# State-space part of the third block: step sizes and decays made once beside the projection, distances on ScalarE, state chain first

## The chip, the cores and the metric

The kernel runs on one core of one Trainium2 chip. The metric is the device time of one execution in microseconds (us), the median of several runs. All data are float32. Five engines work side by side, each through its own instruction queue: TensorE (PE, matmuls), VectorE (DVE), ScalarE (ACT), GpSimd (POOL) and SyncE (SP, which here only issues DMAs).

## The reference, cut to what matters

The program is three blocks after one another on 512 tokens of width 1024. The change lies in the third block, in its bidirectional state-space mixer (`ssd_mixer`): 16 heads of 64 channels, a state of 128, two groups of 8 heads that share the matrices B and C.

```python
xbc = silu(depthwise_conv_centred(xbc, conv_w) + conv_b)        # width 5
y = xh * d_skip
for d in range(2):                                              # forward, backward
    dt = softplus(dt_raw + dt_bias[d]);  a_neg = -exp(a_log[d])
    y = y + ssd_direction(...)                                  # d = 1 on flipped tokens

def step(state, inp):                                           # one chunk of tokens
    cum = cumsum(dt * a_neg)
    seg = cum[t] - cum[s];  decay = exp(seg) where s <= t, else 0
    w = scores[t, s] * decay * dt[s]                            # scores = C B^T
    y_intra = w @ x
    y_inter = (C @ state) * exp(cum)
    state = exp(cum[-1]) * state + (exp(cum[-1] - cum) * dt * x)^T @ B
```

## The kernel before, in words

Channels lie on the 128 partitions and the 512 tokens along the free dimension; the kernel's chunks are P = 128 tokens, so TT = 4 chunks; KT = 8 is both 1024/128 and the number of pairs of heads. Every part is a block: each engine has its instruction list, semaphores order them, and all engines meet at the block's end. Within an engine the order is the one in which the code is written; there is no planner.

`ssd_inputs` makes two norms, then the projection: 20 tiles of 8 matmuls (12 tiles for x, B and C, 8 for the gate z) from weight pieces that `Stream` loads, and one narrow product of 16 columns for `dt_raw` behind them (L2114). ScalarE copies each tile out of PSUM (L2125, L2127), VectorE does the convolution of 5 taps (L2147, L2151), and ScalarE the final Silu (L2132). `ssd_prepare` turns x and B to token-major and makes the scores.

`ssd_direction` runs twice, after that. Its work, on heads in 16 rows first and then on tokens in 128 partitions:

- step sizes and decays: bias, softplus, the running sum by chunk (scan), the rows G (log decay), I (for the state's part of the output), V (weight of a token in the state), in 16x512 tiles, on VectorE with two visits to ScalarE (L2258 to L2310);
- G and I are stored to DRAM (L2238, L2239) and read back broadcast over partitions: one row of G per head into `spread` (L2245), one row of I per head into `ep` (L2251);
- TensorE turns dt, G and V to token-major columns and spreads the chunk decays (L2382, L2385), VectorE copies them out (L2318);
- `xdt` = x times dt, four chunks (L2323); then the chain of three state steps: the weighed input `xw` (L2329), the kept state (L2333), a product per group on TensorE (L2391), and its addition (L2339);
- the pairs of heads: VectorE subtracts the column of G from the spread row and clamps, 4 instructions per head (L2350), ScalarE takes Exp (L2271), VectorE multiplies with the masked scores `gm` (L2371), TensorE makes the state's part (L2400) and the part in the chunk (L2407), VectorE adds both up to y (L2358 to L2360).

VectorE's loop does the differences of pair k + 1, the weights of pair k and the addition of pair k - 1. At the other end of the program, `load_x` loads the small vectors by ScalarE's queue, among them `dt_bias` and `a_log` (L367, L368), and waits for them at its end.

## Time and profile before

| | us |
|---|---|
| median of 3 runs (lowest to highest) | 4182.87 (4182.28 to 4185.58) |
| span of the profiled execution | 4179.0 |
| median less that span | 3.9 |
| projection, first TensorE record to the end of the dt product | 2624.7 to 2771.7 |
| prepare, first to last instruction | 2780.0 to 2788.5 |
| first direction, first to last VectorE instruction | 2788.8 to 2873.5 |
| second direction, first to last VectorE instruction | 2874.1 to 2956.6 |

The profiled execution has no time of its own beside its span; the 3.9 us are what the median of the other runs has over it. Over the whole span TensorE is busy 87%, VectorE 34%, ScalarE 16%. The parts of the program follow each other, so what a part costs is its own length, whatever these shares say.

### The profile page before, as it was taken

The numbers are of one execution on the slowest core, as the hardware profiler recorded it, in microseconds if no ns is written. First come the engines' busy times: TensorE is split into PE (matmuls) and PEld (weight loads), VectorE is DVE, ScalarE is ACT, GpSimd is POOL, SyncE is SP. The second block draws the span as 40 slices with busy tenths as digits, with TensorE's granted clock in tenths as the row PEclk, the third lists the DMA queues.
The fourth block names the chain that finished last, engine by engine and source line by source line (L and its number), as shares of the span: only waits on it lengthen the run. The fifth ranks groups of instructions, "written<-read, shape, count | busy, mean of one in ns | idle before, by whom it ended". The sixth has DMA issues, their size and how long they took to land. (4 is left out here: it accounts for less than half of the span.)

```text
span 4179.0 us, 31843 instructions
## 1 busy us (share of the span) xinstructions
PE 3652.1 (87%) x11526; PEld 1766.0 (42%) x11526; DVE 1431.0 (34%) x2486; ACT 686.6 (16%) x1281; POOL 231.4 (6%) x247
## 2 busy tenths in 40 slices
PE   7998888999794999999999995964899776899998
PEld 2535443443442443434343442433444666444443
DVE  1017622591324212121212124428442788510111
ACT  1012202011102101010101012122171333110000
POOL 0000003000001000000000001000000454000000
PEclk9995798999996999999999997987899888999999
DMA  2225729121116999999999985102221000212220
GB/s 74 70 77 174 251 64 342 64 77 60 51 65 264 371 408 399 408 399 408 399 409 399 408 334 179 57 21 75 96 81 61 6 6 1 101 61 81 81 73 28
DMA packets 218800, 729.49 MB, mean 175 GB/s; under 512 B 16208, under 2 KB 26977, under 8 KB 183879
## 3 DMA queue, kind: packets, MB, share of 16 engines
q1 hardware_dynamic: 178124, 628.30, 39.7%
q10 hardware_dynamic: 28394, 55.66, 3.8%
q0 software_dynamic: 12176, 44.11, 3.0%
q8 instruction: 68, 1.11, 0.1%
q14 instruction: 38, 0.30, 0.0%
HBM read 678.33 MB, written 49.69 MB: 174 GB/s over the span
## 5 line engine op out<-in xcount | busy, mean ns | idle before, releaser
L1739 PE MATMUL bank<-moe_gu,all_hT 128*128 128x512 f32 x1088 | 472.2, 595 | 0.0
L1216 PE MATMUL bank<-all_hT,early_w 128*128 128x512 f32 x896 | 389.4, 598 | 11.7 <-ACT all_hT L492 11.7
L1929 DVE TENSOR_TENSOR all_hT<-bank,moe_bias 128x512 f32<-128x512 f32 x51 | 35.3, 691 | 973.5 <-PE bank L1739 682.3
L1739 PEld LDWEIGHTS bank<-moe_gu,all_hT 128*128 128x128 f32 x1088 | 207.6, 191 | 261.3 <-issue 261.3
L1765 PE MATMUL bank<-moe_dn,moe_rows 128*128 128x512 f32 x544 | 262.6, 645 | 46.7 <-DMA moe_dn<-in_w_dn_dram 45.8
L1216 PEld LDWEIGHTS bank<-all_hT,early_w 128*128 128x128 f32 x896 | 171.7, 192 | 229.3 <-issue 226.3
L1752 PE MATMUL bank<-moe_gu,all_hT 128*64 128x512 f32 x1088 | 236.5, 592 | 1.0 <-issue 1.0
L2465 PE MATMUL bank<-all_hT,hin_w 128*128 128x512 f32 x512 | 222.2, 596 | 13.4 <-DMA hin_w<-in_w_in_dram 13.4
L1216 PE MATMUL bank<-all_hT,late_w 128*128 128x512 f32 x512 | 222.6, 598 | 5.8 <-ACT all_hT L492 5.8
L2768 PE MATMUL bank<-hg_qs,hg_ks 128*128 128x128 f32 x896 | 143.0, 313 | 91.4 <-DVE hg_ks L2714 91.4
L1216 PE MATMUL bank<-b_up,late_w 128*128 128x512 f32 x512 | 220.0, 592 | 2.9 <-PEq L135 2.9
L614 PE MATMUL bank<-all_hT,early_w 128*128 128x512 f32 (+3 forms) x432 | 191.8, 606 | 5.0 <-DVE all_hT L470 5.0
L1765 PEld LDWEIGHTS bank<-moe_dn,moe_rows 128*128 128x128 f32 x544 | 110.9, 207 | 188.3 <-issue 187.8
L2768 PEld LDWEIGHTS bank<-hg_qs,hg_ks 128*128 128x128 f32 x896 | 127.0, 220 | 104.5 <-DVE hg_ks L2714 104.5
L1298 DVE SCALAR_TENSOR_TENSOR b_conv<-conv_ya,all_table,b_conv 128x512 f32<-128x512 f32 x240 | 159.1, 746 | 0.0
L2465 PEld LDWEIGHTS bank<-all_hT,hin_w 128*128 128x128 f32 x512 | 97.9, 192 | 136.7 <-issue 123.1
L1216 PEld LDWEIGHTS bank<-all_hT,late_w 128*128 128x128 f32 x512 | 98.1, 192 | 130.3 <-issue 128.7
L1216 PEld LDWEIGHTS bank<-b_up,late_w 128*128 128x128 f32 x512 | 97.2, 190 | 125.6 <-issue 125.6
L1752 PEld LDWEIGHTS bank<-moe_gu,all_hT 128*64 128x64 f32 x1088 | 81.4, 137 | 152.7 <-issue 152.7
L2108 PE MATMUL bank<-all_hT,si_w 128*128 128x512 f32 x320 | 140.0, 601 | 5.8 <-ACT all_hT L492 5.8
L1778 PE MATMUL bank<-moe_dn,all_hT 128*64 128x512 f32 x544 | 122.4, 602 | 6.6 <-DMA moe_dn<-in_w_dn_dram 4.0
L614 PEld LDWEIGHTS bank<-all_hT,early_w 128*128 128x128 f32 (+3 forms) x432 | 71.6, 167 | 123.7 <-issue 121.2
(585 smaller groups left out, 4067.0 us busy)
## 6 DMA issues: line engine op xcount, KB each, us to landing
moe_gu<-in_w_gu_dram SPq DMA_DIRECT2D x136, 2048.0 KB, 21.4
moe_dn<-in_w_dn_dram SPq DMA_DIRECT2D x68, 2048.0 KB, 23.0
early_w<-in_w_in_dram SPq DMA_DIRECT2D x13, 2048.0 KB, 8.0
expert_rows<-conv_zeros POOLq DMA_DIRECT2D x49, 512.0 KB, 20.3
early_w<-in_w_mod_dram SPq DMA_DIRECT2D x12, 2048.0 KB, 8.0
early_w<-in_ada_w_dram SPq DMA_DIRECT2D x12, 2048.0 KB, 7.9
hin_w<-in_w_in_dram SPq DMA_DIRECT2D x10, 2048.0 KB, 8.5
late_w<-in_w_up_dram SPq DMA_DIRECT2D x8, 2048.0 KB, 9.0
```

Source lines behind the costliest of these rows:

```text
L614: mm = nc.tensor.matmul(out, left, right, start=(k == 0), stop=(k == KT - 1))
L1216: mm = nc.tensor.matmul(B[b][:], w[:, k, m * P:(m + 1) * P], src[:, i * KT + k if stacked else k, :], start=(k == 0), stop=(k == KT - 1))
L1298: nc.vector.scalar_tensor_tensor(out=conv[:, k, :], in0=ya[:, k, bass.ds(j, T)], scalar=conv_w[:, k, bass.ds(j, 1)], in1=conv[:, k, :], op ...
L1739: mm = nc.tensor.matmul(B[bank][:], xb2[:, k, :], gu[:, q, kk, col:col + HALF], start=(k == 0), stop=(k == KT - 1))
L1752: mm = nc.tensor.matmul(B[bank][part, :], xb1[:, k % 4, k // 4, :], gu[:, 4 + q, kk, col + h * HALF:col + (h + 1) * HALF], start=(k == 0), ...
L1765: mm = nc.tensor.matmul(B[2 + n][:], hidT2[:, k * P:(k + 1) * P], dn[:, c, j * D + n * HALF:j * D + (n + 1) * HALF], start=(k == 0), stop= ...
L1778: mm = nc.tensor.matmul(B[4][part, :], hidT1[:, j, c, :], dn[:, c, j * D + h * HALF:j * D + (h + 1) * HALF], start=(c == 0 and j == 0), st ...
L1929: after(vec.tensor_tensor(g, gate[:], bias[0], ALU.add), 1)
L2108: mm = nc.tensor.matmul(B[n % 8][:], w[:, k, (n % 4) * P:(n % 4 + 1) * P], hT[:, k, :], start=(k == 0), stop=(k == KT - 1))
L2465: mm = nc.tensor.matmul(B[n][:], left, right, start=(k == 0), stop=(k == KT - 1))
L2768: mm = nc.tensor.matmul(B[n % 4][:, cols], left[:, cols], right[:, cols], start=True, stop=True)
```

## The change

Step sizes and decays move out of `ssd_direction` into a new class `Steps`, which works once for both directions inside `ssd_inputs`. The two directions lie in one tile of 48 partitions, the backward one from partition 32 (`SSD_BACK`); rows 16 to 31 are zero columns. TensorE makes the dt product first, with the weight columns placed twice; the turning comes after tile 10 of the projection. VectorE works out the chain between the norms and the convolution, weighs after the first quarter of it and copies the columns out after the second. GpSimd stores the four groups of rows. The column of G is kept negated, as `shift`.

In `ssd_direction` the rows of G now go straight into the tile `wgt` (8 heads deep); ScalarE takes the absolute value of row plus `shift` (4 instructions per head), and then Exp with scale -1; VectorE only multiplies. The order on VectorE changes: states first, then mask, then `xdt`, then the pairs.

```diff
-            act.wait_ge(to_act, 1)
-            nc.scalar.activation(tmp[:], dt[:], ACT.Abs).then_inc(act_step, 1)
...
             for k in range(KT):
+                act.wait_ge(spread_loaded[k % SLOTS], 32 * (k // SLOTS + 1))
                 for h in (2 * k, 2 * k + 1):
-                    act.wait_ge(seg_made, h + 1)
-                    nc.scalar.activation(seg[:, h % 4, :], seg[:, h % 4, :], ACT.Exp,
-                                         scale=1.0 if d == 0 else -1.0).then_inc(seg_exped, 1)
+                    for c in range(TT):
+                        part = wgt[:, h % (2 * SLOTS), c * P:(c + 1) * P]
+                        last = nc.scalar.activation(part, part, ACT.Abs, bias=shift[:, c, h:h + 1])
+                    last.then_inc(apart, 1)
+                for h in (2 * k, 2 * k + 1):
+                    act.wait_ge(apart, h + 1)
+                    part = wgt[:, h % (2 * SLOTS), :]
+                    nc.scalar.activation(part, part, ACT.Exp, scale=-1.0).then_inc(exped, 1)
                 act.wait_ge(ep_loaded[k % 3], 32 * (k // 3 + 1))
                 nc.scalar.activation(ep[:, k % 3, :], ep[:, k % 3, :], ACT.Exp).then_inc(ep_made, 1)
...
-            def differences(k):
-                for h in (2 * k, 2 * k + 1):
-                    dve.wait_ge(spread_loaded[h % 4], 16 * (h // 4 + 1))
...
+            vec.memset(S[:, order[0], :], 0.0).then_inc(state, 1)
+            state_input(0)
+            state_input(1)
+            kept_state(0)
+            next_state(0)
+            kept_state(1)
+            state_input(2)
+            next_state(1)
+            kept_state(2)
+            dve.wait_ge(loaded, 16)
+            for g in range(SSD_G):
+                tt(gm[:, g, :].rearrange("p (c t) -> p c t", t=P), scores[:, g, :].rearrange("p (c t) -> p c t", t=P),
+                   mask[:].unsqueeze(1).to_broadcast([P, TT, P]), ALU.mult).then_inc(masked, 1)
+            next_state(2)
+            for c in range(TT):
+                values(c)
+            dve.wait_ge(masked, SSD_G)
             for k in range(KT):
-                if k + 1 < KT:
-                    differences(k + 1)
...
+                weigh(k)
                 if k:
                     add_up(k - 1)
             add_up(KT - 1)
```

In the projection, and in the DMA queue of a direction:

```diff
+            steps.multiply(pe, hT, B[7], normed[-1])
             for n in range(TILES):
                 if n % 4 == 0:
                     w = stream.take(pe)
+                if n == 7:
+                    pe.wait_ge(steps.copied, 1)
                 if n >= 8:
                     pe.wait_ge(copied, n - 7)
+                if n == 16:
+                    pe.wait_ge(steps.placed, 4)
...
+                if n == 10:
+                    pe.wait_ge(copied, 10)
+                    steps.turn(pe, B[0], B[1])
...
             for k in range(KT):
+                if k >= SLOTS:
+                    sp.wait_ge(pair_done, k - SLOTS + 1)
                 for h in (2 * k, 2 * k + 1):
-                    if h >= 4:
-                        sp.wait_ge(seg_made, h - 3)
-                    sp.dma_start(spread[:, h % 4, :], G_dram[h:h + 1, :].to_broadcast([P, T])).then_inc(
-                        spread_loaded[h % 4], 16)
+                    sp.dma_start(wgt[:, h % (2 * SLOTS), :], G_dram[h:h + 1, :].to_broadcast([P, T])).then_inc(
+                        spread_loaded[k % SLOTS], 16)
                 if k >= 3:
                     sp.wait_ge(y_added, k - 2)
```

The new parts of `Steps` that stand on VectorE and TensorE (the arithmetic of the chain is that of before, on 48 rows, with the last copies and subtractions done apart for rows 0 to 31 and 32 to 47):

```diff
+    def turn(self, pe, first, second):
+        R = SSD_ROWS
+        pe.wait_ge(self.rows_ready, 1)
+        for i, (bank, rows) in enumerate(((first, self.dt), (first, self.G), (second, self.V))):
+            for c in range(TT):
+                at = ((i % 2) * TT + c) * R
+                self.nc.tensor.transpose(bank[:, at:at + R], rows[:, c * P:(c + 1) * P], self.ident[0:R, 0:R])
+        for c in range(TT):
+            at = (TT + c) * R
+            mm = self.nc.tensor.matmul(second[:, at:at + R], self.ones[0:R, :], self.diag[:, c, :], start=True, stop=True)
+        mm.then_inc(self.turned, 1)
...
+    def weigh(self, dve):
+        vec = self.nc.vector
+        dve.wait_ge(self.from_act, 2)
+        vec.tensor_tensor(self.V[:], self.V[:], self.dt[:], ALU.mult)
...
+    def place(self, dve, first, second):
+        vec, R = self.nc.vector, SSD_ROWS
+        dve.wait_ge(self.turned, 1)
```

`load_x` now issues four small DMAs for `dt_bias` and `a_log` instead of two, ahead of those for `d_skip`, and two more memsets on GpSimd.

The order on ScalarE in the first direction, before (the names are those above; L2271 is the Exp of a pair, L2274 that of `ep`):

```order
L2258 ACTIVATE ssd_tmp<-ssd_dt 16x512
L2260 ACT_TABLE_LOAD
L2260 ACTIVATE ssd_tmp<-ssd_tmp 16x512
L2261 ACTIVATE ssd_neg<-all_a_log 16x1
L2263 ACT_TABLE_LOAD
L2263 ACTIVATE ssd_tmp<-ssd_tmp 16x512
L2266 ACT_TABLE_LOAD
L2266 ACTIVATE ssd_V<-ssd_V 16x512
L2267 ACTIVATE ssd_tmp<-ssd_tmp 16x4
L2271 ACTIVATE ssd_seg<-ssd_seg 128x512 x2
L2274 ACTIVATE ssd_ep<-ssd_ep 128x512
```

And of the change (L2398 is the absolute value, L2403 the Exp of a pair, L2405 that of `ep`):

```order
L2398 ACTIVATE ssd_wgt<-ssd_wgt,b_shift 128x128 x8
L2403 ACT_TABLE_LOAD
L2403 ACTIVATE ssd_wgt<-ssd_wgt 128x512 x2
L2405 ACTIVATE ssd_ep<-ssd_ep 128x512
L2398 ACTIVATE ssd_wgt<-ssd_wgt,b_shift 128x128 x8
L2403 ACTIVATE ssd_wgt<-ssd_wgt 128x512 x2
L2405 ACTIVATE ssd_ep<-ssd_ep 128x512
```

The work on 16 rows is gone from here. A pair has 8 activations more, and the function table is loaded once, in the first pair.

VectorE in the first direction, before, from the weighing of V on:

```order
L2310 TENSOR_SCALAR ssd_diag<-all_ident,ssd_tmp 16x16 x4
L2313 TENSOR_TENSOR ssd_gm<-b_scores,ssd_mask 128x512 x2
L2318 COPY ssd_dT<-bank 128x64
L2318 COPY ssd_GT<-bank 128x64
L2318 COPY ssd_WT<-bank 128x64
L2318 COPY ssd_CD<-bank 128x64
L2323 TENSOR_TENSOR ssd_xdt<-b_ycat,ssd_dT 128x1024 x4
L2325 MEMSET ssd_S 128x1024
L2329 TENSOR_TENSOR ssd_xw<-b_ycat,ssd_WT 128x1024
L2333 TENSOR_TENSOR ssd_S<-ssd_S,ssd_CD 128x1024
L2339 TENSOR_TENSOR ssd_S<-ssd_S,bank 128x512 x2
L2329 TENSOR_TENSOR ssd_xw<-b_ycat,ssd_WT 128x1024
```

And of the change, from the direction's first instruction on:

```order
L2456 MEMSET ssd_S 128x1024
L2421 TENSOR_TENSOR ssd_xw<-b_ycat,b_WT 128x1024 x2
L2428 TENSOR_TENSOR ssd_S<-ssd_S,b_CD 128x1024
L2436 TENSOR_TENSOR ssd_S<-ssd_S,bank 128x512 x2
L2428 TENSOR_TENSOR ssd_S<-ssd_S,b_CD 128x1024
L2421 TENSOR_TENSOR ssd_xw<-b_ycat,b_WT 128x1024
L2436 TENSOR_TENSOR ssd_S<-ssd_S,bank 128x512 x2
L2428 TENSOR_TENSOR ssd_S<-ssd_S,b_CD 128x1024
L2467 TENSOR_TENSOR ssd_gm<-b_scores,ssd_mask 128x512 x2
L2436 TENSOR_TENSOR ssd_S<-ssd_S,bank 128x512 x2
L2439 TENSOR_TENSOR ssd_xdt<-b_ycat,b_dT 128x1024 x4
L2445 TENSOR_TENSOR ssd_wgt<-ssd_wgt,ssd_gm 128x512 x4
```

The input `xw` of a later state step stands ahead of the addition of the step before, and `xdt` stands behind the chain instead of ahead of it.

TensorE in the projection of the change (before, L2108 was one run of 160 with the 8 of L2114 behind it):

```order
L446 MATMUL bank<-b_ycat,all_ones 128x512 x2
L2121 MATMUL bank<-all_hT,st_wd 48x512 x8
L2250 MATMUL bank<-all_hT,si_w 128x512 x88
L2130 MATMUL bank<-all_ident,st_dt 128x48 x4
L2130 MATMUL bank<-all_ident,st_G 128x48 x4
L2130 MATMUL bank<-all_ident,st_V 128x48 x4
L2133 MATMUL bank<-st_diag,all_ones 128x48 x4
L2250 MATMUL bank<-all_hT,si_w 128x512 x72
```

The 16 turning instructions, which stood in each direction, stand once between tiles 10 and 11.

## Rows read from the trace of the kernel before

**Rows 1.** The table of stretches (us long, busy us by engine, granted clock, DMA)
```profile
core 0: us, PE busy (x) PEld busy (x) DVE busy (x) ACT busy (x) POOL busy (x), PEclk, DMA share, GB/s
...
2634.00:2771.00 137.00, 137.00 (x320) 59.04 (x319) 37.45 (x60) 13.10 (x21) 0.00 (x0) 1.00 0.15 47
...
2833.00:2840.00 7.00, 5.02 (x25) 4.39 (x25) 6.39 (x28) 4.11 (x8) 0.00 (x0) 0.50 0.47 158
2840.00:2874.00 34.00, 21.34 (x168) 18.41 (x168) 32.63 (x78) 10.47 (x17) 0.00 (x0) 0.93 0.32 107
```

**Rows 2.** VectorE in order of time, first direction before its pairs (start, us)
```profile
2788.82 0.47 DVE L2284 TENSOR_SCALAR ssd_dt<-b_dt_raw,all_dt_bias 16x512 f32<-16x512 f32 x1 [5.59 <-PEq L2167]
...
2811.08 4.63 DVE L2323 TENSOR_TENSOR ssd_xdt<-b_ycat,ssd_dT 128x1024 f32<-128x1024 f32 x4
...
2816.70 1.16 DVE L2329 TENSOR_TENSOR ssd_xw<-b_ycat,ssd_WT 128x1024 f32<-128x1024 f32 x1
...
2822.12 1.22 DVE L2329 TENSOR_TENSOR ssd_xw<-b_ycat,ssd_WT 128x1024 f32<-128x1024 f32 x1
...
2827.29 1.22 DVE L2329 TENSOR_TENSOR ssd_xw<-b_ycat,ssd_WT 128x1024 f32<-128x1024 f32 x1
...
2833.18 3.22 DVE L2350 TENSOR_SCALAR ssd_seg<-ssd_spread,ssd_GT 128x128 f32<-128x128 f32 x16
```

**Rows 3.** VectorE in order of time, pairs of heads and the directions' ends
```profile
2836.32 1.28 DVE L2371 TENSOR_TENSOR ssd_wgt<-ssd_seg,ssd_gm 128x512 f32<-128x512 f32 x2
...
2848.06 1.81 DVE L2350 TENSOR_SCALAR ssd_seg<-ssd_spread,ssd_GT 128x128 f32<-128x128 f32 x8
2849.79 1.28 DVE L2371 TENSOR_TENSOR ssd_wgt<-ssd_seg,ssd_gm 128x512 f32<-128x512 f32 x2
2850.99 0.68 DVE L2358 TENSOR_TENSOR ssd_ep<-bank,ssd_ep 128x512 f32<-128x512 f32 x1
...
2872.81 0.69 DVE L2360 TENSOR_TENSOR b_ycat<-b_ycat,ssd_ep 128x512 f32<-128x512 f32 x1
2874.06 0.47 DVE L2284 TENSOR_SCALAR ssd_dt<-b_dt_raw,all_dt_bias 16x512 f32<-16x512 f32 x1 [0.56 <-PEq L2213]
...
2919.83 1.28 DVE L2371 TENSOR_TENSOR ssd_wgt<-ssd_seg,ssd_gm 128x512 f32<-128x512 f32 x2
...
2955.89 0.69 DVE L2360 TENSOR_TENSOR b_ycat<-b_ycat,ssd_ep 128x512 f32<-128x512 f32 x1
```

**Rows 4.** ScalarE in order of time, first direction
```profile
2835.93 1.14 ACT L2271 ACTIVATE ssd_seg<-ssd_seg 128x512 f32<-128x512 f32 x2
...
2851.44 0.63 ACT L2274 ACTIVATE ssd_ep<-ssd_ep 128x512 f32<-128x512 f32 x1 [0.91 <-DMA ssd_ep<-h_rows]
```

**Rows 5.** ScalarE groups by line and shape, whole span (busy us, mean ns, idle)
```profile
L2132 ACT ACTIVATE b_xbc<-b_xbc,all_table 128x512 f32<-128x512 f32 x12 | 7.4, 705 | 0.0
...
L1020 ACT ACTIVATE att_pr<-att_L,att_peak 128x128 f32<-128x128 f32 x6 | 2.4, 402 | 8.6 <-DVE att_peak L992 8.6
```

**Rows 6.** TensorE in order of time, projection and first direction
```profile
2624.74 139.99 PE L2108 MATMUL bank<-all_hT,si_w 128*128 128x512 f32 x320 [5.83 <-ACT all_hT L492]
...
2807.22 0.61 PE L2382 MATMUL bank<-all_ident,ssd_dt 16*128 16x16 f32 x4 [19.33 <-DVE ssd_diag L2310]
...
2808.53 1.86 PE L2385 MATMUL bank<-ssd_diag,all_ones 16*128 16x16 f32 x8
...
2833.20 2.08 PE L2400 MATMUL bank<-b_xbc,ssd_S 128*128 128x128 f32 x8 [0.85 <-DVE ssd_S L2339]
2837.06 2.88 PE L2407 MATMUL bank<-ssd_wgt,ssd_xdt 128*64 128x128 f32 x16 [1.78 <-DVE ssd_wgt L2371]
```

**Rows 7.** DMA issues of the first direction, median us to landing
```profile
ssd_spread<-h_rows SPq DMA_DIRECT2D x16, 256.0 KB, 3.7
```

**Rows 8.** ScalarE in order of time, the program's start
```profile
13.98 0.47 ACTq L368 DMA_DIRECT2D all_a_log<-in_a_log_dram  x1
...
29.83 1.28 ACT L480 ACT_TABLE_LOAD   x1 [7.81 <-PEq L300]
```

More of the change, by code:

```diff
@@ L2072, in ssd_inputs @@
+def ssd_inputs(core, stream, hT, conv_w, conv_b, zs, xbc, normed, steps):
     nc = core.nc
@@ L2121, in _ @@
                 n.scalar(act)
+            steps.take(act, B[7])
+            steps.logs(act)
             for n in range(TILES):
@@ L2139, in _ @@
             nc.vector.memset(raw[:, :, PAD + T:], 0.0).then_inc(padded, 1)
+            steps.vector(dve)
             dve.wait_ge(padded, 2)
@@ L2153, in _ @@
                             op0=ALU.mult, op1=ALU.add).then_inc(convolved if j == SSD_CONV - 1 else tap, 1)
+                if q == 0:
+                    steps.weigh(dve)
+                if q == 1:
+                    steps.place(dve, B[0], B[1])
 def ssd_pieces(w_in):
@@ L2325, in _ @@
[L2325 to L2330 removed]
+            by_head = lambda ap: ap.rearrange("p (h e) -> p h e", e=SSD_DH)
+            spread_out = lambda ap: ap.unsqueeze(2).to_broadcast([P, H, SSD_DH])
@@ L2338, in _, with values, weigh @@
                     cols = slice(g * 512, (g + 1) * 512)
[L2339 to L2343 removed]
+                    tt(S[:, nxt, cols], S[:, nxt, cols], B[g][:], ALU.add).then_inc(state, 1)
+            def values(c):
+                tt(by_head(xdt[:, c, :]), by_head(x_tm[:, c, :]), spread_out(dT[:, c, :]), ALU.mult).then_inc(dt_weighed, 1)
+            def weigh(k):
                 for h in (2 * k, 2 * k + 1):
[L2345 to L2352 removed]
+                    dve.wait_ge(exped, h + 1)
+                    part = wgt[:, h % (2 * SLOTS), :]
+                    tt(part, part, gm[:, h // 8, :], ALU.mult).then_inc(weights, 1)
             def add_up(k):
```

278 lines of the change are left out of this document (148 added, 130 removed).

## The prediction

> **What bounds the kernel now.** I read the page first: the parts of the program follow each other, so the shares of the whole span decide nothing, and a part costs its own length. The table of stretches then shows who works in each part that the change touches. In the projection TensorE is busy all 137.0 of 137 us at a granted clock of 1.00 (2.4 GHz), while VectorE has 37 us of work and ScalarE 13 [rows 1]: two engines are nearly idle beside it. In the pairs of heads VectorE has 32.6 us of 34, TensorE 21.3 and ScalarE 10.5 [rows 1], so VectorE sets that pace.
>
> Next the directions in order of time. The first one starts at 2788.82, its first weights at 2836.32, and its last addition ends at 2872.81 + 0.69 = 2873.50 [rows 2, 3]. That is a head of 47.5 us in which no head's weights are made, and a tail of 37.2 us with the eight pairs. TensorE waits 19.33 us in that head for the small rows [rows 6]. The second direction runs from 2874.06 over 2919.83 to 2956.58 [rows 3]: 45.8 and 36.8 us. Together 167.3 us.
>
> In the tail a pair costs VectorE 1.73 us of differences (2848.06 to 2849.79), 1.20 of weights (to 2850.99) and three additions of 0.72, some 5.0 in all [rows 3].
>
> **What the change removes, adds and moves.**
>
> *The chain of step sizes and decays.* It fills the head from 2788.82 to 2811.08, 22.3 us, masks and column copies with it [rows 2], and the same again in the second direction. It moves beside the projection. There it starts when the dt product, now first, has been copied. With 48 rows in place of 16 an instruction of 512 columns should take what it takes now, since the partitions work side by side; a few are doubled by the split at partition 32. So the chain is ready about 20 to 25 us after the dt product, while tile 3 of the projection ends 4 x 6.86 = 27 us after it (137.0 us is 20 tiles, less a little, [rows 1]). The convolution starts in earnest only with tile 3, so VectorE loses nothing. The weighing stands behind 16 + 4 convolution steps and is wanted by TensorE after tile 10, at 75 us: over 30 us to spare. ScalarE has three table loads more, beside a 13-us load in 137. This term costs 0 while that cover holds. Uncovered it would be the 22 us again, once.
>
> *The dt product.* Eight matmuls of 512 columns move from the end to the start; 48 output rows cost as 16 do. Cost 0: tile 0 was the one that paid for the low clock (139.99 us against 137.0 for 160 matmuls, [rows 6, 1]), now the dt product pays that.
>
> *The turning.* It ran from 2807.22 to 2810.39, 3.2 us for one direction [rows 6], beside nothing. It now stands once in TensorE's stream, where every microsecond counts, with 48 columns in place of 16 but at a clock that is full when it begins. Bounds 1.5 and 6 us (half of the row, and the row plus the 3.0 that a start at the low clock cost the projection); I take 3.0. The end of the projection, the Silu behind it and `ssd_prepare` all move back by this.
>
> At this place the Trainium skill has a rule that speaks against the change. Its page "TensorE: Matmul & The Clock Gate", section "Part 4: PE-mode transpose", says that transposes don't count as work for the clock. By it the turning could drop the clock for the tiles behind, and the term would be near its upper bound; no row shows turning inside dense matmuls, so the sum stays with the middle.
>
> *The head of a direction.* What is left, from the rows: the memset 0.83; the first state step as before, 2816.70 to 2822.12, 5.4 us; the second and third were 5.2 and 5.9 (2822.12 to 2827.29 to 2833.18), but each began with its input of 1.16, which now is made ahead while TensorE works, so 4.0 and 4.7. The masks (1.27) stand in the wait for the last product. Then `xdt`, 4.63 [all rows 2]. Sum 0.8 + 5.4 + 4.0 + 4.7 + 4.6 = 19.5 us to the first weights. The rows of G and I are in DRAM long before, so the first transfers leave at once, and ScalarE has three pairs ready by then.
>
> *The pairs.* VectorE keeps 1.2 + 2.16 = 3.4 us a pair. ScalarE gets 8 activations of 128x128 with a column as bias. Its pace: 12 of 128x512 with such a column take 7.4 us and 0.705 each, so 0.61 from start to start; the 128x128 one takes 0.402 against 0.705, so 0.30 less [rows 5], which leaves 0.31 from start to start. Bounds: 0.20 (the pair of Exp without a column starts 0.51 apart, [rows 4], less the same 0.30) and 0.40 (no overlap). I take 0.30, between the two and nearest to the row with a column. A pair then costs ScalarE 8 x 0.30 + 3 x 0.52 + about 0.15 of waits on itself = 4.1 us. That is more than VectorE's 3.4 and less than the 5.0 of now.
>
> Two things delay the start of the pairs. TensorE is at half clock there (0.50, [rows 1]): 2.08 + 2.88 for the first pair [rows 6], so the first addition ends at 19.5 + 5.0 + 2.2 = 26.7. And ScalarE stands before the fourth `ep`, whose slot is free only with that addition: 3.4 us from an addition's end to the Exp (2848.06 to 2851.44, [rows 3, 4]), to 30.7. The spread rows of pair 4 are issued behind that `ep`, at 27.8 and 28.4, and take up to 3.7 [rows 7]: there at about 31.5. From then: absolute values and Exp of pair 4 to 35.0; the spread rows of pair 5, issued one addition later, hold it to 36.8 and its Exp to 40.3; pairs 6 and 7 follow by 4.1, to 48.5. Then weights 1.2, two additions 4.3: the direction ends at 54.0 less the overlap of the first Exp with the first weight, 0.6, so about 53.4. I take 53.
>
> The second direction is the same: 53. Saved 84.7 + 82.5 - 106 = 61.2 us.
>
> The Trainium skill, "ScalarE: Activation LUTs", section "Rules for kernel authors", tells to keep additions on VectorE, and this one moves them away. The rows agree that the place is dearer, 2.4 us a pair against 1.73. By that rule alone the pair would be slower; it isn't, as long as ScalarE had nothing else to do. The same page's section "What ACT_TABLE_LOAD costs" gives 280 ns + 0.833 ns a column less 93 of overlap, 0.29 us for 128 columns, by which the pair would be 4.05 us.
>
> *The program's start.* Two more DMA issues of about 0.4 us (0.47 for one, [rows 8]) stand ahead of the last ones, for which the next block, at 29.83, may wait: 0 to 1.5, I take 0.8.
>
> **Sum.** -61.2 + 3.0 + 0.8 = -57.4 us. The profiled span of 4179.0 becomes 4121.6; the runs lie 3.9 over that span, so the median of 4182.87 becomes 4125.5.
>
> **The rivals.** What one measurement of this kernel can tell from no change is about 0.2%, 8.4 us.
>
> *ScalarE is slower than I take it* (activations of 0.40 without overlap, and a wait on itself between groups): 5.5 us a pair, more than now. Only the last four pairs hang on it: 31.5 + 4 x 5.5 + 5.5 = 59 us a direction, 12 more than above for both, 4138. For it: the row of 0.402. Against: the starts 0.61 apart at 0.705. Chance 18%.
>
> *TensorE and the transfers are no brake*: VectorE's 3.4 us a pair holds all along, 19.5 + 2.4 + 8 x 2.16 + 6 x 1.2 + 1.5 = 48 us, 10 less for both, 4115. For it: only the first pairs of now are at half clock. Chance 13%.
>
> *The chain isn't hidden*: a wait of TensorE for the rows or the columns, in VectorE's order behind the convolution. It would cost up to the chain's 22 us, 4148. For it: VectorE's order is fixed, and a late tile delays the rest. Against: 30 us to spare. Chance 6%.
>
> *Slower than before*: the narrow first product or the turning leaves TensorE's clock at 1.2 GHz in the projection. Each tile at half clock costs 6.86 us more; from the ninth of the 20 on this eats the gain, and all 20 would give 4126 + 137 = 4263. Against it: the clock came up within the first tile after a pause of 5.8 us [rows 6], and in the pairs, full of waits, it is 0.93 [rows 1]. Chance 2%.
>
> **How the numbers follow.** The forecast has 61%, and its own range is 4118 to 4133. The likeliest gives 4125.5. The range for 8 in 10 takes in most of the first two rivals: 4113 to 4139. Faster by over 0.2% is every case but the last and a part of the one before it, with all that I don't see: 97%; within 0.2% 1%; slower 2%.
>
> **What would show it.** Right: both directions take 50 to 56 us, with ScalarE 80% busy or more from the fifth pair on; in the projection TensorE has one gap or stretch of about 3 us after tile 10 and stays at 1.00; the first weights come 19 to 20 us after the memset. Wrong in the head: TensorE's products of the chain are no longer followed at once by the additions. Wrong in the pairs: starts of the 128x128 activations at 0.20 or 0.40, or ScalarE waiting for the spread rows at each pair. Wrong in the cover: TensorE waiting at tile 10, 11 or 16. A span above 4150 would say that a part outside the directions has changed.

## The result: 4122.99 us, and the profile after

The change ran in 4122.99 us (median of 4 runs, 4120.87 to 4126.83) against 4184.23 for the kernel before (4 runs beside them): ratio 0.9854, 95% interval 0.9842 to 0.9867. The profiled execution took 4121.28 us with a span of 4119.5, 59.5 less than before. The forecast was 4125.5.

The stretches of the kernel after; columns as in [rows 1]. The first three are the projection up to the turning, the turning with what follows it, and the rest; then `ssd_prepare`, the head of the first direction up to its `xdt`, its tail, and the head of the second direction up to its `xdt`.

```profile
2634.00:2709.50 75.50, 75.50 (x176) 33.23 (x176) 39.02 (x62) 12.98 (x20) 2.09 (x4) 1.00 0.18 58
2709.50:2718.50 9.00, 9.00 (x38) 5.02 (x38) 2.33 (x7) 0.59 (x1) 0.00 (x0) 1.00 0.00 0
2718.50:2773.00 54.50, 54.50 (x129) 23.98 (x127) 11.09 (x17) 6.05 (x9) 0.00 (x0) 1.00 0.12 39
2781.70:2791.40 9.70, 8.65 (x56) 8.47 (x56) 3.26 (x8) 6.64 (x12) 0.00 (x0) 0.75 0.00 0
2791.50:2805.00 13.50, 7.42 (x12) 2.53 (x12) 12.74 (x16) 8.50 (x22) 0.00 (x0) 0.87 0.78 219
2809.50:2843.20 33.70, 23.76 (x192) 20.66 (x192) 26.30 (x41) 20.05 (x56) 0.00 (x0) 0.94 0.31 102
2844.20:2859.00 14.80, 9.49 (x12) 3.02 (x12) 12.82 (x16) 10.08 (x30) 0.00 (x0) 0.65 0.75 200
```

TensorE stays busy and at 1.00 through the projection, as before it. What is new stands in the first stretch: VectorE has 39.0 us of work there, the chain and the convolution together, and still nearly half of its time is free. In the tail of the first direction ScalarE now works 20.1 us of 33.7, where it had 10.5 of 34 [rows 1]. The granted clock differs between the heads: 0.87 in the first direction, 0.65 in the second.

VectorE in order of time: the end of the chain in the projection, then the first direction and the beginning of the second. Columns as in [rows 2].

```profile
2634.59 0.48 DVE L2165 TENSOR_SCALAR st_dt<-st_dt,all_dt_bias 48x512 f32<-48x512 f32 x1 [6.91 <-ACT st_dt L2138]
...
2652.01 0.68 DVE L2186 TENSOR_TENSOR st_V<-st_tmp,st_G 32x512 f32<-32x512 f32 x1
...
2673.27 0.67 DVE L2191 TENSOR_TENSOR st_V<-st_V,st_dt 48x512 f32<-48x512 f32 x1
...
2791.54 0.91 DVE L2456 MEMSET ssd_S<- 128x1024 f32 x1 [6.56 <-PEq L2313]
2792.37 2.29 DVE L2421 TENSOR_TENSOR ssd_xw<-b_ycat,b_WT 128x1024 f32<-128x1024 f32 x2
...
2797.13 0.69 DVE L2436 TENSOR_TENSOR ssd_S<-ssd_S,bank 128x512 f32<-128x512 f32 x1 [0.62 <-PE bank L2486]
...
2800.13 1.28 DVE L2436 TENSOR_TENSOR ssd_S<-ssd_S,bank 128x512 f32<-128x512 f32 x2
...
2804.99 4.62 DVE L2439 TENSOR_TENSOR ssd_xdt<-b_ycat,b_dT 128x1024 f32<-128x1024 f32 x4
2809.53 2.49 DVE L2445 TENSOR_TENSOR ssd_wgt<-ssd_wgt,ssd_gm 128x512 f32<-128x512 f32 x4
...
2816.47 1.29 DVE L2445 TENSOR_TENSOR ssd_wgt<-ssd_wgt,ssd_gm 128x512 f32<-128x512 f32 x2
...
2819.84 1.29 DVE L2445 TENSOR_TENSOR ssd_wgt<-ssd_wgt,ssd_gm 128x512 f32<-128x512 f32 x2
...
2824.99 1.29 DVE L2445 TENSOR_TENSOR ssd_wgt<-ssd_wgt,ssd_gm 128x512 f32<-128x512 f32 x2 [1.80 <-ACT ssd_wgt L2403]
...
2842.47 0.69 DVE L2453 TENSOR_TENSOR b_ycat<-b_ycat,ssd_ep 128x512 f32<-128x512 f32 x1
2844.24 0.91 DVE L2456 MEMSET ssd_S<- 128x1024 f32 x1 [1.07 <-DVEq L2361]
```

The chain starts at 2634.59, behind ScalarE's copy of the dt product (2633.98 to 2634.56), and its last row is ready at 2652.69, 18.7 us after the product's end at 2633.95. The weighing stands at 2673.27; TensorE asks for it at 2709.6. In the direction the first state input, at 2792.37, answers to the one at 2816.70 in [rows 2], with only the memset of 2791.54 ahead of it; the first weight comes at 2809.53, where before it took until 2836.32 [rows 3] from a start at 2788.82. The pairs run at 3.37 us while ScalarE is ahead (2816.47 to 2819.84), and from the fifth pair on VectorE waits for ScalarE's Exp (1.80, 0.61, 0.55, 1.46 us). The end is 2843.16.

ScalarE in the same direction:

```profile
2796.47 2.44 ACT L2398 ACTIVATE ssd_wgt<-ssd_wgt,b_shift 128x128 f32<-128x128 f32 x8 [5.48 <-DMA ssd_wgt<-h_rows]
2798.93 1.28 ACT L2403 ACT_TABLE_LOAD   x1
...
2801.80 2.43 ACT L2398 ACTIVATE ssd_wgt<-ssd_wgt,b_shift 128x128 f32<-128x128 f32 x8
...
2805.69 2.43 ACT L2398 ACTIVATE ssd_wgt<-ssd_wgt,b_shift 128x128 f32<-128x128 f32 x8
...
2819.89 0.63 ACT L2405 ACTIVATE ssd_ep<-ssd_ep 128x512 f32<-128x512 f32 x1 [6.84 <-DMA ssd_ep<-h_rows]
2821.93 2.44 ACT L2398 ACTIVATE ssd_wgt<-ssd_wgt,b_shift 128x128 f32<-128x128 f32 x8 [1.40 <-DMA ssd_wgt<-h_rows]
```

Eight absolute values take 2.44 us, a whole pair 3.89 (2801.80 to 2805.69), and the function table is loaded once, while VectorE still works on the states. Then ScalarE stands 6.84 us before the fourth `ep`, whose slot is free only when the first addition ends at 2816.43, and 1.40 us more for the rows of pair 4, which the DMA queue issues behind that `ep`.

TensorE: dt product, turning, and the blocks behind.

```profile
2624.41 9.54 PE L2121 MATMUL bank<-all_hT,st_wd 128*48 128x512 f32 x16 [5.83 <-ACT all_hT L499]
...
2709.61 0.45 PE L2130 MATMUL bank<-all_ident,st_dt 48*128 48x48 f32 x4
...
2710.39 1.05 PE L2133 MATMUL bank<-st_diag,all_ones 48*128 48x48 f32 x8
2711.37 62.07 PE L2250 MATMUL bank<-all_hT,si_w 128*128 128x512 f32 x144
2781.72 5.99 PE L2330 MATMUL bank<-all_ident,b_xbc 128*128 128x128 f32 x32 [8.28 <-PEq L2216]
```

The balance of the 59.5 us, each from the two traces:

| | before | after | difference |
|---|---|---|---|
| start of the program to the projection | 2624.74 | 2624.41 | -0.3 |
| projection to the end of the Silu | 154.93 | 157.00 | +2.1 |
| `ssd_prepare` up to the first direction | 8.85 | 9.82 | +1.0 |
| first direction | 84.7 | 51.6 | -33.1 |
| between the directions | 0.56 | 1.08 | +0.5 |
| second direction | 82.5 | 53.3 | -29.2 |
| all behind | | | -0.4 |

(The rounding of the rows leaves 0.1.) The dearest part of the profile before, the two directions, gave all of the gain; what the moved work costs elsewhere is about 3 us.

### The profile page after: what moved, and what is told of

Read it like the earlier page. It is cut to its first block and busy times, and to the rows that moved or that the text cites. A ratio compares the mean times of both kernels' runs of the same rounds, so it can differ in the third digit from the quotient of the medians.

```text
span 4119.5 us, 31736 instructions
## 1 busy us (share of the span) xinstructions
PE 3641.7 (88%) x11506; PEld 1757.5 (43%) x11506; DVE 1394.0 (34%) x2338; ACT 717.5 (17%) x1402; POOL 234.5 (6%) x254
## 5 line engine op out<-in xcount | busy, mean ns | idle before, releaser
L1936 DVE TENSOR_TENSOR all_hT<-bank,moe_bias 128x512 f32<-128x512 f32 x51 | 35.3, 692 | 973.9 <-PE bank L1746 683.2
```

The lines of the kernel that those rows point to most:

```text
L1936: after(vec.tensor_tensor(g, gate[:], bias[0], ALU.add), 1)
```

## Experiments

All are edits of the changed kernel. Medians move by up to 9 us for reasons that the edited parts don't show (the projection begins anywhere from 2621 to 2632 us in these traces; the parts of e10 are 5.7 us shorter than those of e12, its median is 3.1 us longer), so a single effect is read from the length of its part in the trace, and the ratio to the kernel before stands beside it. Each length comes from one trace. The head is counted from a direction's first VectorE instruction to its first weight, the tail from there to its last addition.

| run | first direction: head / tail | second: head / tail | sum of both | ratio to before |
|---|---|---|---|---|
| before | 47.5 / 37.2 | 45.8 / 36.8 | 167.2 | |
| after | 18.0 / 33.6 | 19.3 / 34.0 | 104.9 | 0.9854 [0.9842, 0.9867] |
| e1, distances on VectorE | 21.1 / 37.8 | 22.4 / 38.6 | 119.9 | 0.9897 [0.9876, 0.9919] |
| e2, old order in the head | 22.5 / 34.4 | 20.9 / 34.0 | 111.9 | 0.9872 [0.9847, 0.9896] |
| e3, chain on its own | 19.3 / 34.3 | 19.3 / 34.7 | 107.6 | 0.9928 [0.9908, 0.9948] |
| e4, light ScalarE | 17.9 / 31.0 | 18.3 / 32.7 | 99.8 | 0.9843 [0.9824, 0.9861] |
| e5, rows ahead of `ep` | 17.9 / 31.3 | 18.3 / 32.5 | 100.0 | 0.9848 [0.9828, 0.9869] |
| e6, eight slots of `ep` | 17.9 / 29.5 | 19.2 / 29.7 | 96.3 | 0.9835 [0.9819, 0.9851] |
| e7, e6 and `xdt` on GpSimd | 18.4 / 29.1 | 18.2 / 28.2 | 93.9 | 0.9822 [0.9803, 0.9841] |
| e8, e7 with all rows at once | 18.4 / 29.1 | 17.4 / 27.4 | 92.3 | 0.9819 [0.9803, 0.9836] |
| e9, three steps more | 15.6 / 27.4 | 19.3 / 29.8 | 92.1 | 0.9837 [0.9823, 0.9851] |
| e10, turning at the end | 17.3 / 34.2 | 18.3 / 34.2 | 103.9 | 0.9863 [0.9847, 0.9879] |
| e11, two pairs deep | 18.0 / 44.4 | 18.3 / 45.0 | 125.6 | 0.9922 [0.9907, 0.9937] |
| e12, the change again | 18.0 / 33.9 | 19.2 / 35.3 | 106.5 | 0.9858 [0.9837, 0.9879] |

Parts of one kernel thus agree within about 1.4 us, and the sum of both directions within 1.6 (after and e12).

**The distances back on VectorE** (e1).

```diff
-                        last = nc.scalar.activation(part, part, ACT.Abs, bias=shift[:, c, h:h + 1])
...
+                        last = vec.tensor_scalar(part, part, shift[:, c, h:h + 1], 0.0, ALU.add,
+                                                 ALU.min if d == 0 else ALU.max)
...
+                if k + 1 < KT:
+                    differences(k + 1)
                 weigh(k)
```

> Undoes one part of the change: the distances are made on VectorE again (subtract and clamp, 4 instructions per head, in the tile wgt), ScalarE has only the Exp; chain beside the projection and states first are kept. Main theory: the pairs then go at VectorE's 1.7 + 1.2 + 2.2 = 5.0 us as in the kernel before (tail 37), and the first two pairs' differences (3.2) stand in the head; a direction of 51.6 becomes about 58 and the one of 53.3 about 58, so the program is 10 to 13 us slower than the changed kernel, some 4134, that is 48 to 50 under the kernel before. Rival (hoisting and the new order carry everything, ScalarE gains nothing because it sets the pace itself): within 3 us of the changed kernel, about 4123.

The directions are 15.0 us longer, above the 10 to 13 expected: 6.2 of it in the heads, as expected, and 8.8 in the tails of 37.8 and 38.6, where 37 was expected. One pair on VectorE in e1:

```profile
2816.88 0.68 DVE L2454 TENSOR_TENSOR ssd_ep<-bank,ssd_ep 128x512 f32<-128x512 f32 x1
...
2819.04 1.66 DVE L2440 TENSOR_SCALAR ssd_wgt<-ssd_wgt,b_shift 128x128 f32<-128x128 f32 x8
2820.62 1.28 DVE L2448 TENSOR_TENSOR ssd_wgt<-ssd_wgt,ssd_gm 128x512 f32<-128x512 f32 x2
2821.82 0.68 DVE L2454 TENSOR_TENSOR ssd_ep<-bank,ssd_ep 128x512 f32<-128x512 f32 x1
...
2824.53 1.66 DVE L2440 TENSOR_SCALAR ssd_wgt<-ssd_wgt,b_shift 128x128 f32<-128x128 f32 x8 [0.58 <-DMA ssd_wgt<-h_rows]
```

The differences take 1.6 us of the pair again (2819.04 to 2820.62), and it lasts 4.9 (2816.88 to 2821.82), as in [rows 3]. Ahead of the next one stands a wait of 0.58 for its rows. The dearer place is the better one here, since ScalarE's time was free.

**The order of before in the head** (e2): masks and `xdt` first, then the memset and step by step input, kept part, addition.

```diff
-            state_input(0)
-            state_input(1)
-            kept_state(0)
...
+            for i in range(TT - 1):
+                if i:
+                    dve.wait_ge(u_made, 2 * i)
+                state_input(i)
+                kept_state(i)
+                next_state(i)
```

> Undoes one part: in the head of a direction VectorE works in the order of before again (masks, xdt, memset, then the three state steps one after the other, each with its input first). Main theory: head 1.2 + 4.6 + 0.8 + 5.4 + 5.2 + 5.9 = 23.2 us in place of 18.0, pairs unchanged, so 5 us a direction and 10 in all: about 4133. Rival (the pairs are held back by ScalarE and by the fourth ep anyway, so a later start is made good in the tail): 0 to 3 us slower, about 4124.

The directions are 7.0 us longer (mostly heads of 22.5 and 20.9 against 18.0 and 19.3). Ahead of each stands a wait of its own besides, 1.6 and 1.7 us: the first instruction now needs the mask, whose transfer starts only with the block. Together 10.3. The 10 of the expectation were to come from the heads alone, of 23.2 us each; that the sum fits is in part luck, since the second head gives only 1.6 and the two waits for the mask, which it didn't have, 3.3. In the first two steps VectorE waits about 1.1 and 0.9 us for TensorE's products, much as in the kernel before; in the change these waits are filled by the next input and the masks.

**The chain without its cover** (e3): dt product, chain and turning in a block of their own behind the projection.

```diff
-            steps.multiply(pe, hT, B[7], normed[-1])
...
+def ssd_steps(core, hT, normed, steps):
...
+        @block.tensor
...
+            steps.multiply(pe, hT, B[7], normed)
+            steps.turn(pe, B[0], B[1])
...
+        @block.vector
...
+            steps.vector(dve)
+            steps.weigh(dve)
+            steps.place(dve, B[0], B[1])
```

> The step sizes and decays of both directions are still made once, but in a block of its own behind the projection (dt product, chain, turning, columns, stores), with its weights loaded before. Main theory (the cover of the projection is what the hoist is worth, beside making it once): dt product 6.9 moved, chain 18.7 from the copy to the last row, weighing 2, turning 2 to 3, columns 1.2, block 1 to 2, less the 2.0 that the turning costs now: 22 to 27 us slower than the changed kernel, about 4147. Rival (making it once for two directions is most of the gain, since a part of the chain is waits that other engines would have had anyway): under 15 us slower.

TensorE in e3:

```profile
2776.72 8.47 PE L2121 MATMUL bank<-all_hT,st_wd 128*48 128x512 f32 x16 [8.43 <-PEq L2216]
2806.09 0.66 PE L2130 MATMUL bank<-all_ident,st_dt 48*128 48x48 f32 x4 [20.89 <-DVE st_diag L2193]
...
2810.82 5.10 PE L2342 MATMUL bank<-all_ident,b_xbc 128*128 128x128 f32 x32 [1.51 <-PEq L2289]
```

From the start of the projection to `ssd_prepare` it is 182.2 us, against 157.3 in the change: the cover is worth 24.9, inside the 22 to 27 expected. Most of it is TensorE's wait of 20.89 us for the last row of the chain. The turning, behind that wait and at a granted clock of 0.50, takes 3.2 us instead of 1.8. The directions are 2.7 longer too, half of it in a first head of 19.3, where the three products of the state chain take 9.5 us in place of 7.4.

**A ScalarE that has less to do** (e4): one absolute value over 512 columns per head, without the shift.

```diff
-                    for c in range(TT):
-                        part = wgt[:, h % (2 * SLOTS), c * P:(c + 1) * P]
-                        last = nc.scalar.activation(part, part, ACT.Abs, bias=shift[:, c, h:h + 1])
-                    last.then_inc(apart, 1)
+                    part = wgt[:, h % (2 * SLOTS), :]
+                    nc.scalar.activation(part, part, ACT.Abs).then_inc(apart, 1)
```

> Leaves out the shift by the column: one plain absolute value of 128x512 per head in place of four of 128x128 with a bias column, so ScalarE's pair falls from 3.9 us to 2.6 us; all else as in the changed kernel. Main theory (ScalarE sets the pace of the last four pairs): VectorE's 3.4 us a pair takes over there, each direction 3 to 5 us shorter, 4115 to 4117 in all. Rival (the transfers behind the fourth ep set the pace, whatever ScalarE does): under 3 us in all, 4120 to 4123, with ScalarE waiting for wgt before each of the last four pairs.

The directions take 5.1 us less, between the 6 to 10 of the main theory and the rival's 3. A pair costs ScalarE 2.6 us now, and it only waits longer for what it is sent:

```profile
2815.92 0.63 ACT L2403 ACTIVATE ssd_ep<-ssd_ep 128x512 f32<-128x512 f32 x1 [12.24 <-DMA ssd_ep<-h_rows]
...
2829.28 1.15 ACT L2397 ACTIVATE ssd_wgt<-ssd_wgt 128x512 f32<-128x512 f32 x2 [2.04 <-DMA ssd_wgt<-h_rows]
```

It waits 12.24 us before the fourth `ep`, and 1.3 to 2.0 before the rows of three of the last four pairs. So making ScalarE faster mostly makes it wait; when slots come free is the limit that is left.

**Rows ahead of `ep` in the DMA queue** (e5).

```diff
+            rows_of(0)
+            for k in range(KT):
+                if k + 1 < KT:
+                    rows_of(k + 1)
```

> Changes only the order in SyncE's queue: the rows of G for pair k + 1 are issued ahead of the ep of pair k, for every k; slots and all computing as in the changed kernel. Main theory (after the first addition ScalarE waits 6.8 us for the fourth ep and then 1.4 us for rows that stand behind it in the queue): only the second wait and the one before the last pair go, so 1.5 to 3 us a direction, 3 to 6 in all; tails 31 to 32 in place of 33.6 and 34.0. Rival (ScalarE's pace alone counts behind the fourth pair): under 1 us a direction.

The directions take 4.9 us less, in the expected 3 to 6. ScalarE still stands 7.34 us before the fourth `ep`, but the rows of pair 4 are there when it comes out, and it doesn't wait again.

**Eight slots of `ep`** (e6).

```diff
-            nc, ctx, name, mask=[P, P], xdt=[P, TT, D], xw=[P, 2, D], gm=[P, SSD_G, T], wgt=[P, 2 * SLOTS, T], ep=[P, 3, T],
+            nc, ctx, name, mask=[P, P], xdt=[P, TT, D], xw=[P, 2, D], gm=[P, SSD_G, T], wgt=[P, 2 * SLOTS, T], ep=[P, 8, T],
...
-                if k >= 3:
-                    sp.wait_ge(y_added, k - 2)
+                if k >= 8:
+                    sp.wait_ge(y_added, k - 7)
```

> Changes only the number of slots of ep, 8 in place of 3, so that no ep waits for an addition; rows of G still in 4 pairs of slots. Main theory (the fourth ep's slot holds ScalarE, and by it the second half of the pairs): ScalarE begins pair 4 some 3 us earlier and VectorE waits for it hardly any more; tails 29 to 30, 8 to 9 us less in all. Rival (ScalarE's 3.9 us a pair against VectorE's 3.4 sets the pace whatever it starts with): tails over 32.5, under 3 us less in all.

The directions are 8.6 us shorter, as expected. The gap between them is 2.05 us in place of 1.07: in e6 to e9 GpSimd clears used semaphores there (five instructions of L133, and one more meeting of all engines, L135). The kernel does this once more than 80 are used, and the added ones bring it forward; in the change the same work stands behind the second direction, so it has moved and isn't an added cost. The waits in the first tail of e6 (engine and line, what for, us, times, longest):

```profile
ACT ssd_wgt L2398 <- DMA ssd_wgt<-h_rows: 5.4, 1, 5.4
...
DVE ssd_wgt L2445 <- ACT ssd_wgt L2403: 0.2, 1, 0.2
```

VectorE waits 0.2 us for ScalarE in the seven pairs of this stretch, where it waited 4.4 in the change. The wait before `ep` was thus the brake of the tail, and a ScalarE of 3.89 us a pair is none, if it may run ahead: it works on the fourth pair when the first weight is made, and ends it 4 us later.

**`xdt` on GpSimd** (e7, on e6).

```diff
-            for c in range(TT):
-                values(c)
...
+        @block.gpsimd
+        def _(pool):
...
+            for c in range(TT):
+                nc.gpsimd.tensor_tensor(by_head(xdt[:, c, :]), by_head(x_tm[:, c, :]), ...,
+                                        ALU.mult).then_inc(dt_weighed, 1)
```

> As the one with 8 slots of ep, and xdt (x times dt, 4 instructions of 128x1024) is made by GpSimd from the start of the direction, beside VectorE's state chain, in place of behind it. Main theory (the head is VectorE's own work, 4.6 of its 18 us are xdt, and GpSimd needs 4 x 2.4 = 9.6 us from its 128x512 rows of 1.2): head 13.5, tail 29 to 30, 17 to 19 us less in all than the changed kernel, directions 43 us. Rival (the two engines slow each other, or GpSimd ends later than the chain): head over 16, VectorE's instructions of the chain longer than 1.22.

The main theory failed: it wanted a head of 13.5 us, and it is 18.4; the directions are 11.0 us shorter than in the change, where 17 to 19 was expected, and 8.6 of that is e6's. GpSimd's row, and VectorE's groups in that head in e7 (columns: line, engine, operation, names, shapes, count, then busy us and mean ns, then idle):

```profile
2798.20 12.43 POOL L2478 TENSOR_TENSOR ssd_xdt<-b_ycat,b_dT 128x1024 f32<-128x1024 f32 x4 [136.30 <-POOLq L2313]
```

```profile
L2421 DVE TENSOR_TENSOR ssd_xw<-b_ycat,b_WT 128x1024 f32<-128x1024 f32 x3 | 6.9, 2332 | 0.0
L2428 DVE TENSOR_TENSOR ssd_S<-ssd_S,b_CD 128x1024 f32<-128x1024 f32 x3 | 5.6, 1878 | 0.1
L2436 DVE TENSOR_TENSOR ssd_S<-ssd_S,bank 128x512 f32<-128x512 f32 x6 | 3.9, 680 | 0.2 <-PE bank L2489 0.2
```

The same groups in the change:

```profile
L2436 DVE TENSOR_TENSOR ssd_S<-ssd_S,bank 128x512 f32<-128x512 f32 x6 | 3.9, 682 | 0.7 <-PE bank L2486 0.6
L2428 DVE TENSOR_TENSOR ssd_S<-ssd_S,b_CD 128x1024 f32<-128x1024 f32 x3 | 3.7, 1222 | 0.1
L2421 DVE TENSOR_TENSOR ssd_xw<-b_ycat,b_WT 128x1024 f32<-128x1024 f32 x3 | 3.5, 1196 | 0.0
```

While GpSimd works, VectorE's instructions that read two operands from SBUF take up to 2.92 us in place of 1.22 (means of 2332 and 1878 ns). Those with one operand in PSUM (L2436) stay at 0.68. Behind GpSimd's end at 2810.63 the same L2428 takes 1.23 again, and in the second direction, where GpSimd needs 10.42 us for its four, it is 2.92 beside it and 1.22 behind. The 4.6 us taken away from VectorE come back as 5.4 of stretch. VectorE waits only 0.19 us for TensorE's products in that head, so the stretch is its own.

**All rows at once** (e8, on e7): eight pairs of rows have a slot of their own, and `ep` has five slots.

```diff
-    SLOTS = 4
+    SLOTS = 8
...
-                if k >= 3:
-                    sp.wait_ge(y_added, k - 2)
+                if k >= 5:
+                    sp.wait_ge(y_added, k - 4)
```

> As the one before, but all 16 rows of G have a slot of their own, so their transfers wait for nothing, and ep has 5 slots. Main theory (with xdt off VectorE the pairs start earlier than ScalarE is ready, and its pairs 4 to 7 wait for rows whose slot is free only with the first products): ScalarE works through without a wait, tails 29 to 29.5, 0 to 3 us less in all than with 4 pairs of slots. Rival (more transfers at the start delay the first ones): the first absolute value starts later than 5 us into the direction and nothing is won.

Tails of 29.1 and 27.4, the expected 29 to 29.5 in one and 1.6 less in the other; ScalarE works through all eight pairs at 3.89 us without a wait. The sum of the directions is 1.6 us below that of e7, in the expected 0 to 3. Its median is 4107.54 us (4102.71 to 4113.06), ratio 0.9819 [0.9803, 0.9836]: it is faster than the change as a whole program too, since the two intervals stand apart.

**Three steps more** (e9, on e6): turning behind the last tile, and `xdt` of the first direction made by VectorE in `ssd_prepare`, where it has time.

```diff
+            pe.wait_ge(copied, TILES - 2)
+            steps.turn(pe, B[0], B[1])
...
+            for c in range(TT):
+                dve.wait_ge(copied, 2 * c + 2)
+                nc.vector.tensor_tensor(by_head(xdt[:, c, :]), by_head(x_tm[:, c, :]), ...,
+                                        ALU.mult).then_inc(skipped, 1)
```

> Three steps more on the changed kernel: ep in 8 slots; xdt of the first direction made by VectorE in ssd_prepare, where it waits (one xdt tile for both directions); the turning and the copies of its columns behind the last tile of the projection, under ScalarE's 7.4 us of Silu. Main theory (VectorE's own work is the bound in a direction, and its waits in front of it are free room): first direction head 13.4 and tail 29.5, 43 us; second as with 8 slots, 48 to 49; the projection to the end of the Silu 155 in place of 157.0; ssd_prepare 9.8 us as now. In all 14 to 16 us under the changed kernel, about 4108. Rival (ssd_prepare becomes longer by what it takes, or ScalarE isn't ready for the earlier pairs): 9 to 10 us, first direction over 46.

The first direction is 4.4 us shorter than in e6 (43.0 against 47.4), and `ssd_prepare`, at 9.1, isn't longer. By their parts (the directions with the gap between them, the projection and `ssd_prepare`) it is 14.7 us shorter than the change, as expected; the median, 4112.64 where about 4108 was expected, is 8.9 below that of e12, and the ratio isn't below e6's. The head is 15.6 where 13.4 was expected. VectorE in e9:

```profile
2790.89 4.62 DVE L2348 TENSOR_TENSOR b_xdt<-b_ycat,b_dT 128x1024 f32<-128x1024 f32 x4
...
2802.65 0.69 DVE L2438 TENSOR_TENSOR ssd_S<-ssd_S,bank 128x512 f32<-128x512 f32 x1 [0.89 <-PE bank L2488]
...
2807.27 0.69 DVE L2438 TENSOR_TENSOR ssd_S<-ssd_S,bank 128x512 f32<-128x512 f32 x1 [0.94 <-PE bank L2488]
...
2811.73 0.69 DVE L2438 TENSOR_TENSOR ssd_S<-ssd_S,bank 128x512 f32<-128x512 f32 x1 [0.72 <-PE bank L2488]
```

Taking 4.62 us out of the head shortens it by 2.3: TensorE's three products take 3.78, 3.75 and 3.59 us at a granted clock of 0.54, against 3.41, 1.96 and 1.95 in e6, and VectorE waits 0.89, 0.94 and 0.72 for them.

**The turning at the end** (e10).

```diff
-                if n == 10:
-                    pe.wait_ge(copied, 10)
-                    steps.turn(pe, B[0], B[1])
+            pe.wait_ge(copied, TILES - 2)
+            steps.turn(pe, B[0], B[1])
```

> Changes only the place of the turning: behind tile 19 in place of tile 10, with the copies of its columns after the whole convolution. Main theory (in the stream it costs its own 2.0 us and nothing of the clock, since the clock stays at 1.00 around it): the projection to the end of the Silu 155 in place of 157.0, the rest as in the changed kernel. Rival (the turning costs the tiles behind it some clock, too): more than 2.5 us are won.

From the start of the projection to the end of the Silu it is 154.63 us, 2.4 less than in the change and 0.3 less than before: the turning is all that had made the projection longer, and behind the last tile it is hidden by the Silu. `ssd_prepare` is 8.91 us again, with a granted clock of 0.84. The median, 4124.67, is not below that of e12, so the gain is read from the parts alone. TensorE's projection in e10 and the first line of the turning behind it:

```profile
2638.72 137.60 PE L2248 MATMUL bank<-all_hT,si_w 128*128 128x512 f32 x320
2776.25 0.45 PE L2130 MATMUL bank<-all_ident,st_dt 48*128 48x48 f32 x4
```

**Two pairs deep** (e11): `SLOTS = 2`, as deep as the kernel before.

> Changes only the depth of the tile wgt: 2 pairs of heads (4 rows, as the kernel before had) in place of 4. Main theory (the longer way row transfer, absolute value, Exp, weight, product pays only with depth): a pair then waits for the product two pairs back, 4.5 us of transfer + 2.4 + 1.1 + 1.3 + 1.6 = 10.9 us for two, 5.4 a pair; tails 41 to 44 in place of 34, 15 to 20 us slower in all, about as slow as with the distances on VectorE or slower. Rival (ScalarE's own 3.9 us a pair is the pace, the transfers are hidden with 2 pairs as well): tails up to 36.

The only edit is the number of slots. The directions take 20.7 us more, 19.2 more than in e12, at the edge of the 15 to 20 expected (the median is 28.2 above e12's); the tails are 44.4 and 45.0, a little above 41 to 44. Waits in the first tail:

```profile
ACT ssd_wgt L2398 <- DMA ssd_wgt<-h_rows: 19.1, 4, 12.3
DVE ssd_wgt L2445 <- ACT ssd_wgt L2403: 15.2, 6, 5.4
```

ScalarE waits 19.1 us for rows, 12.3 of them before pair 2, whose slot is free only with the first product; VectorE then waits 15.2 us for ScalarE. Besides pair 2 it waits 3.39 and 3.17 us before two of the later ones.

**The change again** (e12), as a measure of what a part's length is worth.

> The changed kernel unchanged, on the same chip as the three others, as their base: 4118 to 4127 us, directions 51 to 54, tails 33.5 to 34.5, projection to the end of the Silu 157.

The median is 4121.58 us, ratio 0.9858 [0.9837, 0.9879]. The second direction, 54.6, and its tail, 35.3, are a little above the 51 to 54 and 33.5 to 34.5 expected.

## Why the prediction was right, point by point

*The chain costs nothing beside the projection.* Right: 18.7 us from the dt product's end to the last row, a little under the 20 to 25 forecast, and 35 us to spare before TensorE asks. An instruction on 48 rows takes what it took on 16 (0.68 us for either where two tiles are multiplied); TensorE has no wait at tile 7, 10 or 16. e3 shows that the cover is what counts: 24.9 us without it. It also shows that only a part of the gain was hiding: made apart, once for both directions, the chain costs those 24.9, where the heads before held 22.3 twice.

*The dt product.* Right: 9.54 us in the place of the first tile's 10. The projection as a whole is no longer for it (e10: 154.63 against 154.93).

*The turning, +3.0.* The total of +3.0 fits by luck. The prediction put all of it in TensorE's stream, and there it is 1.8 to 2.4; the rest stands in `ssd_prepare`, for which it had no term. In the stream it costs 1.76 us on TensorE, 1.97 in the spacing of ScalarE's copies (8.83 us from 2709.71 to 2718.54, against 6.86 for a tile), 2.4 by e10. The other 0.9 stands in `ssd_prepare`: in the four kernels that don't turn amid the projection (before, e3, e9, e10) it takes 8.85 to 9.07 us, in the nine others that can be compared 9.6 to 9.8, with the first 32 products at 5.8 to 6.0 in place of 5.1 to 5.3 and the granted clock at 0.75 to 0.77 in place of 0.82 to 0.84. In every trace the longer `ssd_prepare` thus goes with a turning amid the projection; by what way it reaches a block 70 us later isn't shown. During the turning and right behind it the granted clock was 1.00. What the Trainium skill says in "TensorE: Matmul & The Clock Gate", section "Part 4: PE-mode transpose", that transposes don't count as work for the clock, may be so; no tile behind these 2 us ran slower.

*The start, +0.8.* Not seen: the block after `load_x` begins at 29.34, 0.5 us earlier than in [rows 8]. The two DMA issues more are hidden: ScalarE's own first work stands 0.73 us later (16.68 against 15.95), the block doesn't. The term lies just outside its bounds of 0 to 1.5.

*The head, 19.5.* 18.0 and 19.3, where 19 to 20 was to show that the prediction is right: the first lies under it. In the first direction memset 0.83, first step 5.45 (2792.37 to 2797.82), second 3.6, third 3.6, `xdt` 4.5; forecast were 0.8, 5.4, 4.0, 4.7 and 4.6. (The 0.8 and the masks' 1.27 are right, but stand in none of the rows that the prediction names.) Of the 1.5 too much 1.1 is in the third step, where TensorE's product was faster than VectorE's masks. In the second direction the clock is lower, the second product takes 3.75 us, and its step 4.6.

*ScalarE, 0.30 us from start to start and 4.1 a pair.* 2.44 us for eight, and 3.89. Right, so the first rival (0.40, 4138) fell. ScalarE is busy 95% from the fifth pair on, as the prediction asked. By the rate in the Trainium skill, "ScalarE: Activation LUTs", section "What ACT_TABLE_LOAD costs", the estimate for 128 columns is 0.29 from start to start, and the trace, with 2.33 us from the first of eight to the Exp behind them, agrees. The rule of the same page's section "Rules for kernel authors", to keep additions on VectorE, doesn't hold for this kernel: e1, which does so, is 15.0 us slower.

*The start of the pairs.* Forecast: first addition done at 26.7 us from the memset, fourth `ep` begun at 30.1 (26.7 + 3.4; the 30.7 of the prediction is the end of its Exp), rows of pair 4 at 31.5, end at 53.4. Measured in the first direction: 24.9, 28.4, 30.4, 51.6. The 3.4 us from addition to `ep` are 3.46, and the transfer of the rows a median of 4.2 instead of 3.7 (the prediction read this median as the most that one takes). One wait was wrong: ScalarE was to be held before pair 5 until 36.8, but began it at 34.3 without a wait, and waited 0.80 before pair 7 instead. The mechanism is shown by e6, where the wait before `ep` and 8.6 us go, and by e5 from the other side. The second rival (no brake, 10 us less for both) is about what e6 made of the kernel (4115.84); it was a good account of another depth of slots.

*The sum.* -62.3 for the directions where -61.2 was forecast, +3.0 in the projection and `ssd_prepare`, the +3.0 of the forecast, -0.3 for the start's +0.8, and +0.5 between the directions and -0.4 behind them, of which the prediction had nothing. The errors are small and each has its own row: -59.5 against -57.4. They don't all point one way, so a part of the closeness of the sum is luck.

*What the parts are worth.* Taken out one at a time: cover of the chain 24.9 (27.6 with the directions), four pairs of rows in place of two 20.7, distances on ScalarE 15.0, order of the head 10.3. The depth of the slots, which the prediction didn't price by itself, is the second largest: with distances on ScalarE and two pairs the directions take 125.6 us (e11), with distances on VectorE and four pairs 119.9 (e1). Whether depth alone helps a kernel with VectorE's pace of 5.0 was not tried.

## What to carry to other kernels

Work that depends on nothing of its own part belongs beside the nearest long part that leaves its engines idle, and the price of what must stand in that part's own stream is read at the clock there, not at the clock of its old place. An instruction that is dearer on another engine is cheaper if that engine can run ahead, and how far it may run ahead is set by the slots and by the order of the DMA queue that fills them: count for each slot which instruction frees it, before the engine's speed is blamed. Before an operation is given to GpSimd, look where VectorE's operands lie at that time.
